# First attention's norms on TensorE: square sums as two one-pass products, the Newton step on VectorE

## What is computed

```python
q = rms_norm((rms_norm(x, ln_g) @ q_w).reshape(b, s, 8, 2, 64), q_norm_g)
k = rms_norm((rms_norm(x, kv_ln_g) @ kv_w)[..., :1024].reshape(b, s, 8, 2, 64), k_norm_g)
p = softmax(q @ k.T * scale + bias)            # causal, for both halves c of a head
attn = p[:, :, 0] - lam * p[:, :, 1]
o = rms_norm(attn @ v, subln_g) * (1.0 - lam_init)      # over the 128 values of a head
out = o.reshape(b, s, 1024) @ out_w
```

## Time and profile before

| | |
|---|---|
| time of the program, 3 runs | median 2049.0 us (2048.68 to 2049.46) |
| profiled execution | span 2047.5 us from first to last instruction; its own time is not listed apart from the runs, whose median lies 1.5 us above the span |
| TensorE, VectorE, ScalarE, GpSimd busy | 99%, 70%, 45%, 3% of the span |
| mean granted TensorE clock | 0.998 of full |

### The profile page before, as it was taken

One profiled execution on the slowest core, in us unless ns is written; L12 is line 12 of the kernel. 1 busy time (PEld: TensorE's weight loads), 2 busy tenths in 40 slices (PEclk: granted clock), 3 DMA queues, 4 the chain that ended last, 5 costly groups with the idle time before them and its releaser, 6 DMA issues.

```text
span 2047.5 us, 26858 instructions
## 1 busy us (share of the span) xinstructions
PE 2026.5 (99%) x10268; PEld 1635.1 (80%) x10268; DVE 1424.9 (70%) x2093; ACT 927.6 (45%) x1601; POOL 63.3 (3%) x132
## 2 busy tenths in 40 slices
PE   9999999999999999999999999999999999999998
PEld 7887878788888887787778888888777777777787
DVE  7788898777775446566577777447877867566664
ACT  5577775344443234455454444224443332444531
POOL 0000001000000001222000000000000000000000
PEclk9999999999999999999999999999999999999999
DMA  5322222233232333111132332333222224111132
GB/s 177 121 73 73 72 82 63 93 96 100 92 102 81 99 108 114 52 62 38 56 112 94 94 101 83 101 99 104 83 83 77 78 82 165 53 52 52 52 103 83
DMA packets 56225, 179.46 MB, mean 88 GB/s; under 512 B 6287, under 2 KB 9487, under 8 KB 55992
## 3 DMA queue, kind: packets, MB, share of 16 engines
q1 hardware_dynamic: 52416, 167.80, 26.2%
q10 hardware_dynamic: 3704, 10.30, 1.5%
HBM read 175.95 MB, written 4.74 MB: 88 GB/s over the span
## 4 chain that ended last, share of the span: by engine, by line
PE 50%; DVE 1%; ACT 1%; DMA 0%; issue 0%; DVEq 0%
PE bankpair L290 14%; PE bankpair L294 14%; PE bankpair L291 14%; PE bankpair L1532 1%; PE bankpair L1564 1%; PE bankpair L1544 1%; PE bankpair L1400 1%; PE bankpair L1388 1%; PE bankpair L1476 0%; PE bankpair L526 0%; PE bankpair L1457 0%; DMA weight_ring<-up_dram 0%; PE bankpair L1407 0%; DVE residual L2191 0%; PE bankpair L1560 0%; ACT L1726 0%
## 5 line engine op out<-in xcount | busy, mean ns | idle before, releaser
L290 PE MATMUL bankpair<-scaled_in_high,weights_high 128*128 128x512 f32 x1856 | 743.8, 401 | 1.8 <-DVE scaled_in_low L999 0.7
L291 PE MATMUL bankpair<-scaled_in_low,weights_high 128*128 128x512 f32 x1856 | 723.5, 390 | 0.0
L314 ACT ACTIVATE weights_high<-weight_ring 128x1024 fp32r<-128x1024 f32 (+3 forms) x344 | 334.0, 972 | 339.7 <-DMA weight_ring<-down_dram 148.6
L294 PE MATMUL bankpair<-scaled_in_high,weights_low 128*128 128x512 f32 x1856 | 463.0, 389 | 0.0
L325 DVE TENSOR_TENSOR weights_low<-weight_ring,weights_high 128x1024 fp32r<-128x1024 f32 (+3 forms) x344 | 384.1, 1125 | 57.4 <-ACT weights_high L314 47.8
L290 PEld LDWEIGHTS bankpair<-scaled_in_high,weights_high 128*128 128x128 f32 x1856 | 348.7, 188 | 83.0 <-issue 6.5
L291 PEld LDWEIGHTS bankpair<-scaled_in_low,weights_high 128*128 128x128 f32 x1856 | 348.8, 188 | 75.5 <-issue 5.7
L294 PEld LDWEIGHTS bankpair<-scaled_in_high,weights_low 128*128 128x128 f32 x1856 | 348.4, 188 | 72.5
L290 PE MATMUL bankpair<-gated_high,weights_high 128*128 128x512 f32 x448 | 175.1, 391 | 1.9 <-DVE gated_low L2629 1.2
L291 PE MATMUL bankpair<-gated_low,weights_high 128*128 128x512 f32 x384 | 149.4, 389 | 0.0
L589 DVE SCALAR_TENSOR_TENSOR conv_rows<-padded_rows,params,conv_rows 128x512 f32<-128x512 f32 x176 | 131.8, 749 | 7.0 <-ACT conv_rows L558 3.8
(11 more groups left out here) (396 smaller groups left out, 2396.4 us busy)
## 6 DMA issues: line engine op xcount, KB each, us to landing
weight_ring<-up_dram SPq DMA_DIRECT2D x88, 512.0 KB, 3.5
weight_ring<-w_in_dram SPq DMA_DIRECT2D x70, 512.0 KB, 3.5
weight_ring<-in_w_dram SPq DMA_DIRECT2D x40, 512.0 KB, 3.6
weight_ring<-down_dram SPq DMA_DIRECT2D x32, 384.0 KB, 3.1
weight_ring<-kvq_dram SPq DMA_DIRECT2D x24, 512.0 KB, 3.5
weight_ring<-down_dram SPq DMA_DIRECT2D x32, 320.0 KB, 2.8
weight_ring<-out_a_dram SPq DMA_DIRECT2D x8, 512.0 KB, 3.6
weight_ring<-out_b_dram SPq DMA_DIRECT2D x8, 512.0 KB, 3.6
```

Source lines behind the costliest of these rows:

```text
L290: nc.tensor.matmul(bank, WH[:, high_slot, cell], high, start=(k == 0), stop=False)
L291: nc.tensor.matmul(bank, WH[:, high_slot, cell], low, start=False, stop=False)
L294: mm = nc.tensor.matmul(bank, WL[:, slot, cell], high, start=False, stop=(c == last_k))
L314: nc.scalar.activation(WH[:, (PART0[name] + k) % SLOTS, 0:n], RAW[:, b % SLOTS, 0:n], ACT.Copy).then_inc(high_ready, 1)
```

## The change

The squares are split too: ScalarE squares the tile twice, once into a one-pass type (high) and once whole, and GpSimd subtracts the two (low). TensorE then sums with a block of ones (`ONES_R`, or `HALF_R` with two diagonal blocks of ones for k and q) as weights and the 512-wide high and low squares as moving data, so that each sum arrives at once on all partitions that need it, and no transposes follow. ScalarE's first root is 512 wide (logarithm, then exponential), and the Newton step is three 512-wide instructions on VectorE (`newton`), the first of which reads the sums in PSUM. GpSimd's small steps are gone. The k and q roots lie in the buffer `conv_rows`, that of the output in `reciprocals`, the Newton temporary in `floor`.

```diff
-        SQ = sb("squares", [P, 2, T])
-        ACC = sb("square_sums", [P, T])
+        ONES_R = sb("ones_for_parts", [P, P], F32R)[:, :]
+        HALF_R = sb("half_ones_for_parts", [P, P], F32R)[:, :]
+        with ExitStack() as whole_squares:
+            SQ = whole_squares.enter_context(nc.sbuf_tensor("squares", [P, 2, T], F32))
+            ACC = whole_squares.enter_context(nc.sbuf_tensor("square_sums", [P, T], F32))
+        SQ_R = sb("squares_low", [P, 2, T], F32R)
+        ACC_R = sb("out_squares_low", [P, T], F32R)
...
-        MEAN, LOGS, ROOT, NEWT = ([at(NT, 2) for _ in range(2)] for _ in range(4))
-        INV = [buf.rearrange("p (c d) -> p c d", d=P) for buf in (EMB, RDB)]
-        OMEAN, OLOG, OROOT, ONEWT, ORMS = (at(NT) for _ in range(5))
+        ROOT = [CV[:, 0, :], CV[:, 1, :]]
+        OROOT = RDB[:, :]
+        NEWT = EMB[:, :]
+        ROOT_R = [HIGH_R[:, 0, :], HIGH_R[:, 1, :]]
...
             def head_sums(h, which):
 
-                pe.wait_ge(hsq, 2 * h + which + 1)
+                pe.wait_ge(hsl, 2 * h + which + 1)
                 if which == 0 and h >= 1:
                     pe.wait_ge(v_ready, h)
+                if which == 1 and h >= 1:
+                    pe.wait_ge(hs_read[1], h)
                 if which == 1 and h >= 3:
-                    pe.wait_ge(oh_ready, h - 2)
-                if which == 1 and h >= 1:
-                    pe.wait_ge(qn_ready, h)
-                for c in range(NT):
-                    at = 8 * which + 2 * c
-                    mm = nc.tensor.matmul(BANK[6 + which][:, at:at + 2], SQ[:, which, c * P:(c + 1) * P],
-                                          const("half_ones")[:, 0:P:64], start=True, stop=True)
-                mm.then_inc(hss, 1)
-
-            def spread_norm(h, which):
-
-                pe.wait_ge(inv_ready, 2 * h + which + 1)
-                if which == 1 and h >= 2:
-                    pe.wait_ge(oroot_ready, h - 1)
-                for c in range(NT):
-                    mm = nc.tensor.transpose(BANK[6 + which][:, c * P:(c + 1) * P],
-                                             INV[which][:, c, :], IDENT)
-                mm.then_inc((kb_done, qb_done)[which], 1)
-
-            def spread_out(h):
-                pe.wait_ge(ro_ready, h + 1)
-                pe.wait_ge(qn_ready, min(h + 3, AH))
-                for c in range(NT):
-                    mm = nc.tensor.transpose(BANK[7][:, c * P:(c + 1) * P], ORMS[:, c:c + 1].to_broadcast([P, P]), IDENT)
-                mm.then_inc(outb_done, 1)
...
             def out_sums(h):
-                pe.wait_ge(ob_ready, 2 * h + 2)
-                pe.wait_ge(qn_ready, min(h + 2, AH))
-                pe.wait_ge(root_ready, min(2 * h + 6, 2 * AH))
+                pe.wait_ge(osl, h + 1)
+                pe.wait_ge(hs_read[1], min(h + 3, AH))
                 if h >= 1:
-                    pe.wait_ge(oh_ready, h)
-                for c in range(NT):
-                    mm = nc.tensor.matmul(BANK[7][:, c:c + 1], SQO[:, c * P:(c + 1) * P], ONES[:, 0:1], start=True, stop=True)
-                mm.then_inc(oss_done, 1)
+                    pe.wait_ge(os_read, h)
+                nc.tensor.matmul(BANK[7][:, :], ONES_R, OUT_R[:, :], start=True, stop=False)
+                nc.tensor.matmul(BANK[7][:, :], ONES_R, ACC_R[:, :], start=False, stop=True).then_inc(oss_done, 1)
...
             norm_sum(pe, 2)
+            pe.wait_ge(ones_r, 2)
             tile(0, 1)
             tile(0, 2, range(0, KD // 2))
             head_sums(0, 0)
             tile(0, 2, range(KD // 2, KD))
-            spread_norm(0, 0)
             cells_of(1, 0, 6)
             head_sums(0, 1)
             turn_v(0)
...
             logs = Count(act, log_step)
             log_exp_tables()
+            act.wait_ge(gemm_done, TILE0["down0"] + KD)
+            nc.scalar.activation(ONES_R, ONES[:, :], ACT.Copy).then_inc(ones_r, 1)
+            nc.scalar.activation(HALF_R, const("half_ones"), ACT.Copy).then_inc(ones_r, 1)
             high_query(act, HIGH_FIRST, KD)
...
                 if h >= 1:
                     act.wait_ge(hss, 2 * h + which - 1)
-                nc.scalar.activation(SQ[:, which, :], U[:, 0, 3:3 + T] if which == 0 else QN[h % 2],
-                                     ACT.Square).then_inc(hsq, 1)
-
-            def first_root(mean, log, root, sums, scale):
-                logs.step(nc.scalar.activation(mean, sums, ACT.Identity, bias=EPSC[:, 0:1], scale=scale))
-                logs.step(nc.scalar.activation(log, mean, ACT.Ln))
-                return nc.scalar.activation(root, log, ACT.Exp, scale=-0.5)
+                    act.wait_ge((kq_ready, qn_ready)[which], h)
+                raw = U[:, 0, 3:3 + T] if which == 0 else QN[h % 2]
+                nc.scalar.activation(ROOT_R[which], raw, ACT.Square).then_inc(hsq, 1)
+                nc.scalar.activation(SQ[:, which, :], raw, ACT.Square).then_inc(hsq, 1)
+
+            def first_root(root, sums, scale):
+                logs.step(nc.scalar.activation(root, sums, ACT.Ln, bias=EPSC[:, 0:1], scale=scale))
+                return nc.scalar.activation(root, root, ACT.Exp, scale=-0.5)
 
             def inverse(h, which):
                 act.wait_ge(hss, 2 * h + which + 1)
-                if h >= 1:
-                    act.wait_ge(inv_ready, 2 * h + which - 1)
-                sums = BANK[6 + which][:, 8 * which:8 * which + 8].rearrange("p (c n) -> p c n", n=2)
-                first_root(MEAN[which], LOGS[which], ROOT[which], sums, 1.0 / 64).then_inc(root_ready, 1)
+                first_root(ROOT[which], BANK[6 + which][:, :], 1.0 / 64).then_inc(root_ready, 1)
...
                 nc.scalar.activation(OB, BANK[5][:, :], ACT.Copy).then_inc(ob_ready, 1)
+                nc.scalar.activation(OUT_R[:, :], BANK[5][:, :], ACT.Square).then_inc(ob_ready, 1)
                 nc.scalar.activation(SQO, BANK[5][:, :], ACT.Square).then_inc(ob_ready, 1)
...
         def attention_pool(pool):
...
+            def low_squares(h, which):
+                pool.wait_ge(hsq, 2 * (2 * h + which + 1))
+                sq = SQ[:, which, :]
+                nc.gpsimd.tensor_tensor(SQ_R[:, which, :], sq, ROOT_R[which].bitcast(F32), ALU.subtract).then_inc(hsl, 1)
+
+            def low_out_squares(h):
+                pool.wait_ge(ob_ready, 3 * h + 3)
+                nc.gpsimd.tensor_tensor(ACC_R[:, :], SQO, OUT_R[:, :].bitcast(F32), ALU.subtract).then_inc(osl, 1)
...
+            def newton(root, sums, n, read):
+
+                read.step(nc.vector.scalar_tensor_tensor(NEWT, sums, n * EPS, root, ALU.add, ALU.mult))
+                step.step(nc.vector.scalar_tensor_tensor(NEWT, NEWT, -0.5 / n, root, ALU.mult, ALU.mult))
+                step.step(nc.vector.scalar_tensor_tensor(root, NEWT, 1.5, root, ALU.add, ALU.mult))
+
+            def head_root(h, which):
+                dve.wait_ge(root_ready, 2 * h + which + 1)
+                newton(ROOT[which], BANK[6 + which][:, :], 64, hr_read[which])
+
+            def out_root(h):
+                dve.wait_ge(oroot_ready, h + 1)
+                newton(OROOT, BANK[7][:, :], P, or_read)
...
             def k_norm(h):
 
-                dve.wait_ge(kb_done, h + 1)
                 if h >= 2:
                     dve.wait_ge(s_done, NR * (h - 1))
-                kq.step(nc.vector.scalar_tensor_tensor(KN[h % 2], U[:, 0, 3:3 + T], LAM[:, 70:71], BANK[6][:, :],
+                kq.step(nc.vector.scalar_tensor_tensor(KN[h % 2], U[:, 0, 3:3 + T], LAM[:, 70:71], ROOT[0],
                                                        ALU.mult, ALU.mult))
 
             def q_norm(h):
-                dve.wait_ge(qb_done, h + 1)
-                qn.step(nc.vector.tensor_tensor(QN[h % 2], QN[h % 2], BANK[7][:, :], ALU.mult))
+                qn.step(nc.vector.tensor_tensor(QN[h % 2], QN[h % 2], ROOT[1], ALU.mult))
...
                     if r == 0:
+                        if h == 0:
+                            head_root(0, 1)
                         q_norm(h)
...
                         evac(h + 2, 0)
+                    if r >= 1 and h + 1 < AH:
+                        head_root(h + 1, r - 1)
...
                     if r == 0 and h >= 2:
+                        out_root(h - 2)
                         out_norm(h - 2)
```

90 lines of the change are left out of this document (35 added, 55 removed).

## The result

The changed kernel takes **2098.1 us** (median of 4 runs, 2097.7 to 2100.3), the kernel before, run beside it, 2048.8: a ratio of 1.0241, with a 95% interval of 1.0229 to 1.0254. That is 49.3 us slower, where 36 was forecast; the time lies inside the range, near its upper end.

What follows compares the result with a forecast made beforehand. TensorE's instruction stream was taken to bound the kernel. Net of its saving, +15 us to scores (6,0), +8 and +4 at the attention's end, and +9 for the clock gave +36 on 2049.0: 2085 us, range 2066 to 2100.

Steps and rivals of the forecast that it cites:

- What is taken off TensorE: Norm sums and spreads in the attention: 2.55 us a head saved, taken as 2.1 after changes of instruction kind.
- Wait A: Round 2, heads 1 to 5: output sums wait 4.35 us for VectorE's first q Newton instruction to free their PSUM bank.
- Wait B: Round 1's first turned attention, from head 2 on: TensorE waits 0.6 us because the output norm precedes combine on VectorE.
- 2.36 new: VectorE time in us of one norm's three added Newton instructions, here the output norm's ahead of combine in round 0.
- Wait C: Second tile, before head 0: TensorE waits 4.6 us for ScalarE's copies of the ones, behind its table load.
- The clock: Long stalls bring TensorE's clock down: 1.5 us lost at each of six stalls, +9 us; bounds 0 and 5.5 a stall.
- The end of attention: Scores (6,0) to (7,1), where TensorE follows VectorE's chain with three Newton steps: +8 us; +4 more behind it.
- (1): Rival: the clock stays full through the stalls; +27 us, 2076 us; chance 0.22.
- (2): Rival: the stalls are hidden and only TensorE's work counts; -17 us, 2032 us; chance 0.05.
- (3): Rival: output-sum stall shorter, or the end shorter by half, the stall for the ones as said; about 2060 us; chance 0.06.
- (4): Rival: the clock stays low for the whole next run of products; 33 us in place of 9, 2109 us; chance 0.07.
- the sum with the clock: Whole kernel: 27 us of waits and chain plus 9 us for clock falls, +36 us, 2085 us; chance 0.60.

Runs made afterwards that it cites:

- e5: Changed kernel without the 24 Newton steps, norms taken with ScalarE's first root alone: 2044.17 us, ratio 0.9973 to the kernel before.
- e9: Changed kernel with e1, e2, e3, output norms of heads 5 and 6 among those moved earlier, and two VectorE instructions per Newton step instead of three: 2045.02 us.
- e1: Changed kernel with round 2's q Newton step moved ahead of the logits on VectorE: 2067.95 us.
- e3: Changed kernel with GpSimd's q subtraction made to wait for the head's first combine: 2092.77 us.
- e2: Changed kernel with TensorE's wait for the ones moved from the second tile to just ahead of the first head's sums: 2093.82 us.
- e4: Changed kernel with eighteen idle 128x512 products ahead of the output sums in heads 1 to 5: 2086.32 us.
- e11: As e9, with head 7's low parts reordered and, in head 6, head 5's output sums behind that round's cells, turned attention and v product: 2040.42 us.

## Why the prediction came out as it did

- **What is taken off TensorE**: 2.1 us a head taken, 2.45 measured (e5, e9). The 0.4 us deducted for changes of kind was wrong; the rows alone (2.55) were nearly right. 3 us too little over the attention.
- **Wait A**: right in place, cause and size: 4.26 to 4.30 against 4.35. Moving its instructions alone took 30 us off (e1).
- **Wait B**: the step that failed in the middle heads. Place and cause were right, the term "2.36 new" was mis-sized: it took 3.14 (888.54 to 891.68), since GpSimd's subtraction blocks the third Newton instruction for 1 us. The prediction priced the subtraction as GpSimd's time only, and asked of neither what it does to the other. The wait is 0.9 us longer for it in each of heads 2 to 5; with the 1.4 us of head 6, taking the cause away gave 5.3 us (e3).
- **Wait C**: right. 4.1 us against 4.6, and 4.3 us of the total (e2). But at scores (1,0) the kernel is 4.2 us behind, not 2.5. The clock stayed low for 5.1 us of products behind this stall, an estimated 2.6 us lost where 1.5 was taken, and scores (1,0) wait 0.48 us for `q_norm(1)`, whose third Newton instruction was blocked to 1.67 us too.
- **The clock**: the mechanism was right, the size 1.5 us a fall was low: 2.3 on average (e4). The 3 us at the low level that the prediction took were met in head 3 alone (3.0 us, 1.4 lost); elsewhere it was 4.5 to 6.0 us. The bounds 0 and 5.5 held it.
- Together, for heads 2 to 5: 0.9 + 0.8 - 0.35 = 1.35 us a head above the forecast of 4.35; measured 1.4 (5.7).
- **The end of attention**: forecast +8, measured +12.4. The timeline of TensorE from scores (6,0) to (7,1):

```profile
982.83 0.93 PE L724 MATMUL bankpair<-arena 64*128 64x128 f32 x8
...
993.17 0.90 PE L734 MATMUL bankpair<-constants,arena 128*128 128x128 f32 x3 [4.04 <-DVE arena L1086]
...
1003.23 0.77 PE L754 MATMUL bankpair<-out_squares_high,ones_for_parts 128*128 128x512 f32 x1 [4.58 <-issue]
...
1008.83 1.07 PE L724 MATMUL bankpair<-arena 64*128 64x128 f32 x8
...
1013.76 0.50 PE L298 MATMUL bankpair<-query_in_high,weights_high 128*128 128x512 f32 x1 [1.37 <-DVE query_in_low L1099]
...
1020.07 0.50 PE L298 MATMUL bankpair<-query_in_high,weights_high 128*128 128x512 f32 x1 [2.02 <-DVE query_in_low L1099]
...
1021.20 0.92 PE L724 MATMUL bankpair<-arena 64*128 64x384 f32 x4
```

Against the chain laid out from scores (6,0) = 0: turned attention 10.3 for 9.4, output sums 20.4 for 18.3, scores (7,0) 26.0 for 21.9, scores (7,1) 38.4 for 34.0. VectorE shows the first two pieces:

```profile
988.55 1.76 DVE L1038 SCALAR_TENSOR_TENSOR reciprocals<-floor,reciprocals 128x512 f32<-128x512 f32 x1
...
998.68 0.17 DVE L1080 RECIPROCAL arena<-arena 128x2 f32<-128x2 f32 x1 [1.31 <-ACT arena L875]
```

The blocked Newton instruction again, and then `combine(6, 1)`, which waits for ScalarE's exponentials, in ScalarE's order behind `head_out(5)`, which waits for the product with v, run at half clock; the chain had no term for it. The sentence that the clock's fall in head 6 "costs TensorE nothing" was wrong there: the clock fell twice, and from the turned attention to scores (7,0) TensorE's products were half as fast and some of them, those with v above all, stood on the path. How the 4.4 us split between these was not measured one by one. Behind scores (7,1) the forecast was good: head 6's output sums wait 1.25 us for 1.2, head 7's 3.18 for 3.4. e1 and e3 took 2.0 and 1.4 off this stretch, e5, which has no Newton steps, 6.8, and 5.6 us more than before remain in it with none. In e5 the clock's three falls are part of these 5.6 us; what makes its waits longer than before (6.0 against 2.1 us) stays open. ScalarE's 512-wide roots and the third square are suspects that were not tried apart.
- **Rivals**: (1), the clock stays full, fell with e4 and the windows; (2), all hidden (2032), fell, and e11, rebuilt towards it, is still at 2040; (3) fell, A had its full length; (4), low for the whole next run at 5.5 us a stall, fell: full again after 3.0 to 6.0 us of products, at 2.3 us a stall. So the sum with the clock was the right one of the two.
- **How near the total came**: 2085 against 2098.1, two microseconds inside the upper bound. By the table the misses are 1.7 us up to scores (1,0), 0.8 in head 1, 5.6 in heads 2 to 5, 4.4 at the end and 0.7 behind it; the forecast was too low in each of them, though TensorE's saving is in it and was taken too small. The upper bound was worked out from the length of the low clock alone; that it also held the blocked Newton instruction and the longer chain at the end was luck.

That slack of 11 us a head would not help unless the work stood in it was the prediction's main statement, and e1 shows it from the other side: the same instructions ahead of the logits instead of behind them are nearly free.
